# Second layer's recurrence: one 128-column product for both kinds of scores, a third scores buffer, seven parts of each inverse per chunk

## The chip, the cores and the metric

The kernel runs on one core of one Trainium2 chip. The metric is the device time of one launch in microseconds (us): 1906.67 us is the median of three runs before the change. TensorE is the matrix engine, VectorE, ScalarE and GpSimd are the three engines for elementwise work; the profile calls them PE, DVE, ACT and POOL, and TensorE's weight loads PEld.

## What is computed

One inference step of a two-layer recurrent decoder trunk, for a prompt of 512 tokens and 8 samples of 4 tokens each, width 1024. The first layer mixes with GLA and HGRN2, the second with RWKV-7, 16 heads of 64. Each layer also has a SwiGLU block and a gated embedding. The change is in the recurrence of the second layer:

```python
def step(s, inp):
    r_t, lw_t, k_t, v_t, kk_t, a_t = inp
    s_kk = jnp.einsum('bhik,bhk->bhi', s, kk_t)
    s = (s * jnp.exp(lw_t)[:, :, None, :]
         - s_kk[..., :, None] * (kk_t * a_t)[..., None, :]
         + v_t[..., :, None] * k_t[..., None, :])
    return s, jnp.einsum('bhij,bhj->bhi', s, r_t)
```

## The kernel before, in words

The program is one long list of instructions for each engine, with semaphores between them, all written out by hand. Nearly all of the time is in products of 128x128 weights (line 351) that run from the embedding to the last feed-forward block; between the products of the second layer's r, k, v and those of its output weight lies the recurrence, from 1088 us to 1299 us of the span.

The recurrence treats the prompt in chunks of 64 tokens (`CP`), so there are 8, and the samples as a ninth, `SAMPLE`. It is in the form that turns 64 steps into products of matrices. For each chunk m and each of the 16 heads there are two kinds of keys (`keys_p(tile, b)`: b = 1 the removal keys kk·a, b = 0 the keys k) and two kinds of query (`qrF[:, tile, 0]` the kk, `qrF[:, tile, 1]` the r). Their products are the scores; the triangular matrix of removal keys against kk has to be inverted. The work of a chunk is in two pieces.

**The stream** (`pe_stream`, `dve_stream`, `act_stream`, `pool_stream`) is what does not need the state. It is a list of parts, `parts_of(m)`:
- `aT`: 16 products of 64 columns, the scores of the removal keys against kk (line 2452). VectorE takes the first level of the inverse out of them and transposes it (lines 2646 and 2650), ScalarE copies the whole (line 2581).
- `P` and `X` for the levels 2 to 6: the inverse is built by doubling its blocks. P (line 2462, 16 products of 32 columns) waits for ScalarE's copy of the level before; VectorE merges it under a mask (`level_factor`, line 2661, after a transpose on line 2667); X (line 2505, 16 products) waits for that; ScalarE writes it back (line 2615; line 2620 at the last level), and GpSimd makes the copy with the halves swapped (line 2743) that the next transpose reads.
- `A`: 16 products, scores of k against kk (line 2468), which VectorE masks into `sAs` (line 2715).
- `O`: 32 products, both kinds of keys against r (line 2473), which VectorE masks into `sOs` in two instructions (line 2721).
- `vt` and `kt`: transposes of the values and keys (lines 2479 and 2482), copied out by ScalarE and VectorE.

**The chunk** (`pe_chunk` and its like) is what goes through the state: `av` (line 2768), the state against kk (R, line 2776) and against r (oR, line 2783), the inverse applied (U, line 2791), the output from the scores `sOs` (line 2803), the new state (line 2809). After each of these stands a slot, `go_on(0)` to `go_on(6)`, in which `in_chunk` puts parts of streams: "o" is the next part of the stream of chunk n+1, "n" that of chunk n+2. `HEAD` is the number of parts by which the stream n+1 is ahead when chunk n begins. A stream has 15 parts: 8 are done as "n" and 7 as "o". All engines go through the same slots in the same order, each with its own share of a part.

Each stream has two banks of PSUM, streams of even and odd chunks different ones (`bank_of`), so most parts wait until the part before has been read out; P and X use columns apart.

## Time and profile before

| | |
|---|---|
| median of 3 runs | 1906.67 us (1904.36 to 1910.46) |
| the profiled execution: its time, and its span | 1911.56 us, 1909.8 us |
| PE busy | 1761.2 us (92%) |
| PE weight loads busy | 1665.2 us (87%) |
| DVE, ACT, POOL busy | 981.6, 725.0, 217.8 us |
| mean TensorE clock | 0.937 of full |

The span is the time from the first to the last instruction that the profiler saw; the run's time is 1.8 us more. Busy time is a mean over stages of different kinds; the recurrence has windows of its own below. In the profile one 16-product part of fp32 stands as 32 matmul and 32 weight-load records.

### The profile page before, as it was taken

Reading aid. Unit: us, or ns where it says so; the run is one execution under the profiler, and the core shown is the slowest. Engines: PE = TensorE matmul, PEld = TensorE weight load, DVE = VectorE, ACT = ScalarE, POOL = GpSimd, SP = SyncE. Lnnn points to the kernel's source line nnn. Section 1 sums busy time; section 2 is a strip of 40 time slices with the busy share of each in tenths; the row PEclk is TensorE's granted clock in tenths of the full one; section 3 lists DMA queues with packets and bytes.
Section 4 is the critical chain, followed back from the end, with each engine's and each line's share of the span. In section 5 each row is a group of like instructions: output and inputs, shape, how many; then the busy total and the mean of one; then the engine's idle time right before and its main releaser. Section 6 shows DMA issues by size and latency. Waiting matters only on the chain.

```text
span 1909.8 us, 43023 instructions
## 1 busy us (share of the span) xinstructions
PE 1761.2 (92%) x18617; PEld 1665.2 (87%) x18617; DVE 981.6 (51%) x1407; ACT 725.0 (38%) x953; POOL 217.8 (11%) x307
## 2 busy tenths in 40 slices
PE   7999879799999999997999877779899999999997
PEld 6999876799999999997888767765599999999997
DVE  4487775644433444456788544433644442444444
ACT  4353444354522222333466223223445531222243
POOL 1042551000000000120060111112100000000000
PEclk8999989899999999998999878886799999999999
DMA  4321131332332333330222200010143232233321
GB/s 130 82 74 47 55 102 52 89 111 88 92 96 66 88 88 102 88 89 23 79 67 74 73 3 4 4 49 1 32 107 113 86 108 78 68 88 101 88 67 58
DMA packets 234669, 138.95 MB, mean 73 GB/s; under 512 B 4720, under 2 KB 229360, under 8 KB 234528
## 3 DMA queue, kind: packets, MB, share of 16 engines
q1 hardware_dynamic: 226784, 116.73, 21.2%
q0 software_dynamic: 4864, 15.90, 3.3%
q10 hardware_dynamic: 2880, 4.21, 0.6%
q8 instruction: 116, 1.90, 0.4%
q14 instruction: 25, 0.20, 0.0%
HBM read 128.66 MB, written 8.16 MB: 72 GB/s over the span
## 4 chain that ended last, share of the span: by engine, by line
PE 80%; DVE 9%; ACT 4%; issue 3%; POOL 2%; DMA 1%; ACTq 0%; SPq 0%; DVEq 0%; POOLq 0%
PE ps L351 62%; PE ps L1881 2%; PE ps L2505 1%; PE ps L1628 1%; ACT w_head L315 1%; DVE w_rest L320 1%; PE ps L2462 1%; PE ps L1862 1%; PE ps L2803 1%; POOL mix L984 1%; PE ps L1093 1%; PE ps L1169 1%; PE ps L2809 1%; PE ps L1900 1%; PE ps L3004 1%
## 5 line engine op out<-in xcount | busy, mean ns | idle before, releaser
L351 PE MATMUL ps<-x_split,w_head 128*128 128x272 f32 (+1 forms) x5312 | 900.0, 292 | 24.7 <-DVE x_split L1418 8.6
L351 PEld LDWEIGHTS ps<-x_split,w_head 128*128 128x128 f32 x5312 | 763.6, 191 | 38.5 <-issue 27.7
L351 PE MATMUL ps<-x_split,w_rest 128*128 128x272 f32 (+1 forms) x2656 | 555.5, 291 | 0.0
L315 ACT ACTIVATE w_head<-w_raw 128x1024 fp32r<-128x1024 f32 (+1 forms) x205 | 227.1, 1108 | 584.1 <-PE ps L351 566.8
L351 PEld LDWEIGHTS ps<-x_split,w_rest 128*128 128x128 f32 x2656 | 421.4, 191 | 0.0
L320 DVE TENSOR_TENSOR w_rest<-w_raw,w_head 128x1024 fp32r<-128x1024 f32 (+1 forms) x205 | 268.0, 1307 | 171.3 <-ACT w_head L315 171.2
L351 PE MATMUL ps<-hidden_split,w_head 128*128 128x272 f32 x1408 | 233.1, 287 | 0.0
L351 PEld LDWEIGHTS ps<-hidden_split,w_head 128*128 128x128 f32 x1408 | 198.0, 188 | 0.0
L351 PE MATMUL ps<-hidden_split,w_rest 128*128 128x272 f32 x704 | 145.3, 287 | 0.0
L1459 DVE TENSOR_TENSOR hT<-hT,ps 128x544 f32<-128x544 f32 (+1 forms) x40 | 28.8, 721 | 161.1 <-PE ps L351 161.1
L351 PEld LDWEIGHTS ps<-hidden_split,w_rest 128*128 128x128 f32 x704 | 110.0, 188 | 0.0
L1592 DVE TENSOR_TENSOR mix<-mix,ps 128x544 f32<-128x544 f32 x44 | 31.7, 721 | 127.7 <-PE ps L351 127.7
L1588 DVE TENSOR_TENSOR mix<-mix,ps 128x544 f32<-128x544 f32 x44 | 31.7, 721 | 63.8 <-PE ps L351 57.5
L1578 ACT ACTIVATE hidden_split<-mix 128x544 f32 (+1 forms) x44 | 29.0, 659 | 91.3 <-DVE mix L1596 91.3
L1762 POOL DMA_DIRECT2D out_y_prompt<-mix x4 | 2.2, 551 | 483.4 <-ACT mix L1706 483.3
L1598 DVE TENSOR_TENSOR hidden_split<-mix,hidden_split 128x544 f32 (+1 forms) x44 | 31.9, 725 | 42.5 <-ACT hidden_split L1578 42.5
L984 POOL TENSOR_TENSOR mix<-mix 128x256 f32<-128x256 f32 (+1 forms) x36 | 32.0, 890 | 176.6 <-DVE mix L1011 88.8
L1827 POOL DMA_DIRECT2D tables<-in_odd_tables x1 | 0.6, 563 | 449.7 <-PE ps L351 449.7
L1093 PE MATMUL ps<-mix 64*64 64x64 f32 (+1 forms) x896 | 36.6, 229 | 8.1 <-DVE mix L1011 8.1
L315 ACT ACT_TABLE_LOAD x20 | 25.7, 1283 | 40.6 <-PE ps L351 40.6
L1093 PEld LDWEIGHTS ps<-mix 64*64 64x64 f32 (+1 forms) x896 | 30.7, 140 | 11.6 <-DVE mix L1011 9.2
L2462 PE MATMUL ps<-odd_quad 64*64 64x32 f32 x1280 | 32.7, 245 | 7.3 <-issue 5.0
(454 smaller groups left out, 2136.5 us busy)
## 6 DMA issues: line engine op xcount, KB each, us to landing
w_raw<-in_w_ffn_gate SPq DMA_DIRECT2D x44, 512.0 KB, 3.7
w_raw<-in_w_ffn_up SPq DMA_DIRECT2D x44, 512.0 KB, 3.7
w_raw<-in_w_ffn_down SPq DMA_DIRECT2D x32, 704.0 KB, 4.7
w_raw<-in_w_in_even SPq DMA_DIRECT2D x29, 512.0 KB, 3.7
w_raw<-in_w_ple_gate SPq DMA_DIRECT2D x16, 512.0 KB, 3.9
w_raw<-in_w_out_even SPq DMA_DIRECT2D x8, 512.0 KB, 4.0
w_raw<-in_rw_wr SPq DMA_DIRECT2D x8, 512.0 KB, 3.8
w_raw<-in_rw_wk SPq DMA_DIRECT2D x8, 512.0 KB, 3.9
```

The costliest lines, as they stand in the source:

```text
L315: act.activation(wh[:, s, 0:kt * P], raw[:, s, 0:kt * P], ACT.Copy).then_inc(head_ok[s], 1)
L320: dve.tensor_tensor(wl[:, s, 0:kt * P], raw[:, s, 0:kt * P], wh[:, s, 0:kt * P].bitcast(F32), ALU.subtract).then_inc(rest_ok[s], 1)
L351: mm = pe.matmul(ps[:, 2 * s + h, 0:half.stop - half.start], w[:, s, k * P:(k + 1) * P], x[:, k, half], start=first and k == 0, stop=k == ...
L984: pool.tensor_tensor(e[:, :, 0, :], mid, b[:, :, 0, :], ALU.subtract)
L1093: mm = pe.matmul(ps[64 * (c % 2):64 * (c % 2) + CE, b0 + level // 2, at:at + CE], left[:, c * CE:(c + 1) * CE], right[:, c * CE:(c + 1) * CE],
L1459: dve.tensor_tensor(h, h, out2(s), ALU.add).then_inc(bank_free[s], 1)
L1578: act.activation(hid[:, 0, ds(j, 1), :], prod.unsqueeze(1), ACT.Copy).then_inc(hhead_ok, 1)
L1588: dve.tensor_tensor(two(act_out), two(norm_f.rs), out2(0), ALU.mult).then_inc(bank_free[0], 1)
L1592: dve.tensor_tensor(two(prod), two(norm_f.rs), out2(1), ALU.mult).then_inc(bank_free[1], 1)
L1598: dve.tensor_tensor(hid[:, 1, ds(j, 1), :], prod.unsqueeze(1), hid[:, 0, ds(j, 1), :].bitcast(F32), ALU.subtract).then_inc(hrest_ok, 1)
L1881: mm = pe.matmul(ps[:, 2 * s + h, 0:tokens.stop - tokens.start], w[:, s, k * P:(k + 1) * P], x[:, k, tokens], start=first and k == 0, stop ...
L2462: mm = pe.matmul(bank(1 - c)[half(1 - p ^ c), i * CO:(i + 1) * CO], aTs[par][r, swap_cols(c, i)], even_columns(xxs[par][r, swap_cols(c, i) ...
```

## The change

The parts aT, A and O become two. `scores(pe, b, bank)` makes, for one kind of keys, the product against kk and r side by side: the moving operand is `qrF[..., :, tokens]`, 2 x 64 columns. So aT (b = 1) and A (b = 0) are 16 products of 128 columns each, O is no part any more, and a stream has 14 parts. VectorE masks the scores against r in `out_scores`, two instructions of 64 partitions for each kind of keys: for b = 1 directly behind the first transpose of the inverse (named `O{m}_1`, and P of level 2 waits for it), for b = 0 behind the masking of A. As the b = 1 scores are now made two chunks ahead of their use, `sOs` gets a third buffer. HEAD is 7, and the slots are filled anew.

```diff
         aTS, bTS = low2[0][:, 0:P], [low2[0][:, P:2 * P], low2[0][:, 2 * P:3 * P]]
         xTS, xxS, ppS = (low2[1][:, k * P:(k + 1) * P] for k in range(3))
         sAs = [quad[:, 3584:4096], quad[:, 5120:5632]]
-        sOs = [quad[:, 4096:5120], quad[:, 5632:6656]]
+        sOs = [ap.rearrange("p (c x) -> p c x", c=2)[:, :, 0:512] for ap in (
+            quad[:, 4096:5120], quad[:, 5632:6656], mix[:, 25600:28672])]
         vus = [quad[:, at:at + 1024].rearrange("p (i b g v) -> p i b g v", i=4, b=2, g=2) for at in (6656, 7680)]
         sc_sample = mix[:, 25600:26112].rearrange("p (g n t) -> p g n t", g=2, n=4)
         vu_sample = mix[:, SC0 + 1024:SC0 + 1536].rearrange("p (i g v) -> p i g v", i=4, g=2)
...
                 return [("sc", 0), ("P", 2), ("X", 2), ("vt", 0), ("kt", 0)] + [("st", b) for b in range(2, NB)] + [
                     ("rts", 0)]
             parts = [("aT", 0)] + [(kind, level) for level in range(2, LEVELSP + 1) for kind in "PX"]
-            parts += [("A", 0), ("O", 0), ("vt", 0), ("kt", 0)]
+            parts += [("A", 0), ("vt", 0), ("kt", 0)]
             return parts + [("st", 0), ("st", 1)] if m == SAMPLE - 2 else parts
 
-        HEAD = 8
+        HEAD = 7
 
         def part_name(m, kind, x):
             return f"st{x}" if kind == "st" else "rts" if kind == "rts" else f"{kind}{m}_{x}"
...
 
         def in_chunk(streams, n, slot):
 
-            order = ("o", "n", "o", "on", "n", "on", "nononon")[slot]
+            order = ("on", "", "o", "on", "on", "on", "nonon")[slot]
             for who in order:
                 if who == "o" and n + 1 in streams:
                     next(streams[n + 1], None)
...
                 pe.wait_ge(*O1.dve.at("nrm"))
             par, before = m % 2, None if m < 2 else (m - 2, *parts_of(m - 2)[-1])
             tokens = slice(CP * m, CP * m + CP) if m < SAMPLE else slice(TP, T)
+
+            def scores(pe, b, bank):
+                for i, p, c in tile_heads:
+                    out = bank(1 - c)[half(p ^ b), i * 2 * CP:(i + 1) * 2 * CP].rearrange("p (s t) -> p s t", s=2)
+                    mm = pe.matmul(out, keys_p(2 * i + p, b)[half(c), m, :], qrF[half(c), 2 * i + p, :, tokens], start=True,
+                                   stop=True)
+                return mm
+
             for kind, x in parts_of(m):
                 if before is not None and (m == SAMPLE or kind not in ("P", "X")):
                     for by in readers(*before):
...
                 if m == SAMPLE and kind in ("sc", "P", "X", "vt", "kt", "rts"):
                     mm = pe_sample_part(pe, kind, bank)
                 elif kind == "aT":
-                    for i, p, c in tile_heads:
-                        mm = pe.matmul(bank(1 - c)[half(1 - p), i * CP:(i + 1) * CP], keys_p(2 * i + p, 1)[half(c), m, :],
-                                       qrF[half(c), 2 * i + p, 0, tokens], start=True, stop=True)
+                    mm = scores(pe, 1, bank)
                 elif kind == "P":
                     if x == 2:
                         pe.wait_ge(*O2.act.at(f"aT{m}_0"))
                         pe.wait_ge(*O2.dve.at(f"t{m}_2"))
+                        pe.wait_ge(*O2.dve.at(f"O{m}_1"))
                     else:
                         pe.wait_ge(*O2.act.at(f"X{m}_{x - 1}"))
                     for i, p, c in tile_heads:
...
                 elif kind == "X":
                     mm = pe_inverse(pe, m, x, bank)
                 elif kind == "A":
-                    for i, p, c in tile_heads:
-                        mm = pe.matmul(bank(c)[half(p), i * CP:(i + 1) * CP], keys_p(2 * i + p, 0)[half(c), m, :],
-                                       qrF[half(c), 2 * i + p, 0, tokens], start=True, stop=True)
-                elif kind == "O":
-                    for b in range(2):
-                        for i, p, c in tile_heads:
-                            mm = pe.matmul(bank(c)[half(p ^ b), (2 * i + p) * CP:(2 * i + p + 1) * CP],
-                                           keys_p(2 * i + p, b)[half(c), m, :], qrF[half(c), 2 * i + p, 1, tokens], start=True,
-                                           stop=True)
+                    mm = scores(pe, 0, bank)
                 elif kind == "vt":
                     for i in range(KT // 2):
                         at = 17408 + 1024 * i + P * m
...
         def both(m, wide):
             return ps[:, bank_of(m, 0):bank_of(m, 0) + 2, 0:wide]
 
+        def made_scores(m, s):
+            return both(m, 512).rearrange("p c (i s t) -> p c i s t", i=4, s=2)[:, :, :, s, :]
+
+        def out_scores(dve, m, b):
+
+            for p in range(2):
+                r = half(p ^ b)
+                mm = dve.tensor_tensor(sOs[m % 3][r].rearrange("p c (i b t) -> p c i b t", i=4, b=2)[:, :, :, p, :],
+                                       made_scores(m, 1)[r], scP[r, 1, :].unsqueeze(1).unsqueeze(1).to_broadcast([64, 2, 4, CP]),
+                                       ALU.mult)
+            return mm
+
         def act_stream(act, m):
             par = m % 2
             for kind, x in parts_of(m):
...
                         dst = rows_p[:, :, P * m:P * m + P].rearrange("p (b t) x -> p b t x", b=2)
                         src = both(m, 512).rearrange("p b (t x) -> p b t x", t=4)
                     else:
-                        dst = aTs[par].rearrange("p (c x) -> p c x", c=2)
-                        src = both(m, 256)
+                        dst, src = aTs[par].rearrange("p (c i t) -> p c i t", c=2, i=4), made_scores(m, 0)
                     act.activation(dst, src, ACT.Copy).then_inc(*O2.act.done(name))
                 if m < SAMPLE and kind == "P" and x == 2:
                     first_own_rows(act, m)
...
                 dve.wait_ge(*O2.dve.at(f"t{m - 1}_2"))
             dve.copy_predicated(first.rearrange("p (c i t) -> p c i t", c=2, i=4),
                                 level_bits[:, 0:CP].unsqueeze(1).unsqueeze(1).to_broadcast([P, 2, 4, CP]),
-                                both(m, 256).rearrange("p c (i t) -> p c i t", i=4)).then_inc(*O2.dve.done(f"Y{m}"))
+                                made_scores(m, 0)).then_inc(*O2.dve.done(f"Y{m}"))
             dve.wait_ge(*O2.dve.at(f"Y{m}"))
             dve.transpose(xxs[m % 2], first).then_inc(*O2.dve.done(f"t{m}_2"))
+            dve.wait_ge(*O2.act.at(f"aT{m}_0"))
+            if m > 2:
+                dve.wait_ge(*O2.pe.at(f"o{m - 3}"))
+            out_scores(dve, m, 1).then_inc(*O2.dve.done(f"O{m}_1"))
 
         def level_factor(dve, m, level):
 
...
                     elif m == SAMPLE:
                         dve.tensor_tensor(xTS, xTS, ps[:, bank_of(m, 0), 0:P], ALU.add).then_inc(*O2.dve.done(name))
                     elif kind == "A":
-                        dve.tensor_tensor(sAs[par].rearrange("p (c i t) -> p c i t", c=2, i=4),
-                                          both(m, 256).rearrange("p c (i t) -> p c i t", i=4),
-                                          scP[:, 0, :].unsqueeze(1).unsqueeze(1).to_broadcast([P, 2, 4, CP]), ALU.mult).then_inc(
-                            *O2.dve.done(name))
-                    elif kind == "O":
-                        for c in range(2):
-                            mm = dve.tensor_tensor(sOs[par][:, 512 * c:512 * c + 512].rearrange("p (n t) -> p n t", n=8),
-                                                   ps[:, bank_of(m, c), :].rearrange("p (n t) -> p n t", n=8),
-                                                   scP[:, 1, :].unsqueeze(1).to_broadcast([P, 8, CP]), ALU.mult)
-                        mm.then_inc(*O2.dve.done(name))
+                        dve.tensor_tensor(sAs[par].rearrange("p (c i t) -> p c i t", c=2, i=4), made_scores(m, 0),
+                                          scP[:, 0, :].unsqueeze(1).unsqueeze(1).to_broadcast([P, 2, 4, CP]), ALU.mult)
+                        out_scores(dve, m, 0).then_inc(*O2.dve.done(name))
                     else:
                         dst, src = values_in(m, 1)
                         dve.tensor_copy(dst, src).then_inc(*O2.dve.done(name))
...
                 pe_sample_chunk(pe)
                 return
             par, tokens = n % 2, slice(CP * n, CP * n + CP)
-            vu, sA, sO, xT = vus[par], sAs[par], sOs[par], xTs[par]
+            vu, sA, sO, xT = vus[par], sAs[par], sOs[n % 3], xTs[par]
             pe.wait_ge(*O2.dve.at(f"A{n}_0"))
             pe.wait_ge(*O2.dve.at(f"vt{n}_0"))
             pe.wait_ge(*O2.act.at(f"vt{n}_0"))
             for i, p, c in tile_heads:
-                mm = pe.matmul(ps[half(1 - p ^ c), 2 + c, i * NC:(i + 1) * NC], sA[half(p), head_cols(c, i)],
+                mm = pe.matmul(ps[half(1 - p ^ c), 2 + c, i * NC:(i + 1) * NC], sA[half(p), swap_cols(c, i)],
                                vu[half(p), i, p, c ^ p, :], start=i == 0, stop=n == 0, skip_group_check=True)
             mm.then_inc(*O2.pe.done(f"av{n}" if n else "R0"))
             go_on(0)
...
             go_on(3)
             pe.wait_ge(*O2.act.at(f"U{n}"))
             pe.wait_ge(*O2.dve.at(f"U{n}"))
-            pe.wait_ge(*O2.dve.at(f"O{n}_0"))
             pe.wait_ge(*O2.act.at(f"kt{n}_0"))
             if n > 0:
                 pe.wait_ge(*O2.pe.at(f"oR{n}"))
             for i, p, c in tile_heads:
                 g = c ^ p
                 pe.matmul(ps[half(g), 4 + p, 256 + i * CP:256 + (i + 1) * CP], vu[:, i, p, g, :],
-                          sO[:, 512 * c + (2 * i + p) * CP:512 * c + (2 * i + p + 1) * CP], start=n == 0 and i == 0, stop=True,
+                          sO[:, 1 - c, (2 * i + p) * CP:(2 * i + p + 1) * CP], start=n == 0 and i == 0, stop=True,
                           skip_group_check=True)
             go_on(4)
             for i, p, c in tile_heads:
```

How the change moves the work is seen in the order of the instructions. The first place is TensorE in the middle of a prompt chunk of the steady state, from the new state (line 2809 before, 2816 now) to the part that stands last ahead of the next chunk. Before:

```order
L2809 MATMUL ps<-odd_quad,mix 64x64 x16
L2468 MATMUL ps<-mix 64x64 x16
L2462 MATMUL ps<-odd_quad 64x32 x16
L2505 MATMUL ps<-mix,odd_quad 64x32 x16
L2473 MATMUL ps<-mix 64x64 x32
L2462 MATMUL ps<-odd_quad 64x32 x16
L2479 MATMUL ps<-ident,mix 128x128 x4
L2505 MATMUL ps<-mix,odd_quad 64x32 x16
L2482 MATMUL ps<-ident,mix 128x128 x8
L2462 MATMUL ps<-odd_quad 64x32 x16
```

Now:

```order
L2816 MATMUL ps<-odd_quad,mix 64x64 x16
L2448 MATMUL ps<-mix 64x128 x16
L2470 MATMUL ps<-odd_quad 64x32 x16
L2505 MATMUL ps<-mix,odd_quad 64x32 x16
L2479 MATMUL ps<-ident,mix 128x128 x4
L2470 MATMUL ps<-odd_quad 64x32 x16
L2482 MATMUL ps<-ident,mix 128x128 x8
L2505 MATMUL ps<-mix,odd_quad 64x32 x16
```

The 32 products of O are gone, A (now line 2448) has 128 columns, and P of level 5 has moved behind the next chunk's av. The second place is TensorE from av of the next chunk to the output product. Before:

```order
L2768 MATMUL ps<-odd_quad 64x64 x16
L2505 MATMUL ps<-mix,odd_quad 64x32 x16
L2776 MATMUL ps<-mix 64x64 x16
L2452 MATMUL ps<-mix 64x64 x16
L2783 MATMUL ps<-mix 64x64 x16
L2462 MATMUL ps<-odd_quad 64x32 x16
L2791 MATMUL ps<-mix,odd_quad 64x64 x16
L2505 MATMUL ps<-odd_quad,mix 64x32 x16
L2462 MATMUL ps<-odd_quad 64x32 x16
L2803 MATMUL ps<-odd_quad 64x64 x16
```

Now:

```order
L2776 MATMUL ps<-odd_quad 64x64 x16
L2470 MATMUL ps<-odd_quad 64x32 x16
L2448 MATMUL ps<-mix 64x128 x16
L2784 MATMUL ps<-mix 64x64 x16
L2791 MATMUL ps<-mix 64x64 x16
L2505 MATMUL ps<-mix,odd_quad 64x32 x16
L2799 MATMUL ps<-mix,odd_quad 64x64 x16
L2470 MATMUL ps<-odd_quad 64x32 x32
L2810 MATMUL ps<-odd_quad 64x64 x16
```

aT (line 2448 with 128 columns) stands ahead of both products with the state; between its end and P of level 2 (the second half of the row of 32) stand R, oR, X of level 5, U and P of level 6. The third place is VectorE in the same chunk, from the first level of the inverse of chunk n+2 to the masks of A. Before:

```order
L2646 COPY_PREDICATED mix<-odd_levels_on_chip,ps 128x512
L2650 STREAM_TRANSPOSE odd_quad<-mix 128x512
L2667 STREAM_TRANSPOSE odd_quad<-odd_quad 128x512
L2661 COPY_PREDICATED mix<-odd_levels_on_chip,ps 128x8x32
L2881 COPY odd_quad<-ps 64x2x4x64
L2661 COPY_PREDICATED mix<-odd_levels_on_chip,ps 128x128x2
L2715 TENSOR_TENSOR odd_quad<-ps,tables 128x512
L2667 STREAM_TRANSPOSE odd_quad<-odd_quad 128x512
L2661 COPY_PREDICATED mix<-odd_levels_on_chip,ps 128x64x4
```

Now:

```order
L2657 COPY_PREDICATED mix<-odd_levels_on_chip,ps 128x512
L2661 STREAM_TRANSPOSE odd_quad<-mix 128x512
L2558 TENSOR_TENSOR odd_quad<-ps,tables 64x8x64 x2
L2888 COPY odd_quad<-ps 64x2x4x64
L2682 STREAM_TRANSPOSE odd_quad<-odd_quad 128x512
L2676 COPY_PREDICATED mix<-odd_levels_on_chip,ps 128x8x32
L2676 COPY_PREDICATED mix<-odd_levels_on_chip,ps 128x128x2
L2730 TENSOR_TENSOR odd_quad<-ps,tables 128x512
L2558 TENSOR_TENSOR odd_quad<-ps,tables 64x8x64 x2
L2682 STREAM_TRANSPOSE odd_quad<-odd_quad 128x512
L2676 COPY_PREDICATED mix<-odd_levels_on_chip,ps 128x64x4
```

Two masking instructions of 64 partitions (line 2558) stand ahead of the copy of U (2888), and two more between the mask of A (2730) and the transpose and merge of level 3.

## Rows read from the trace of the kernel before

**Rows 1.** The page: busy time, share of the span, instructions, of TensorE
```profile
PE 1761.2 (92%) x18617; PEld 1665.2 (87%) x18617; DVE 981.6 (51%) x1407; ACT 725.0 (38%) x953; POOL 217.8 (11%) x307
```
**Rows 2.** Windows: length, busy (records) of PE, PEld, DVE, ACT, POOL, clock, DMA
```profile
1088.10:1119.60 31.50, 24.01 (x716) 22.00 (x716) 13.94 (x24) 5.82 (x15) 7.25 (x22) 0.50 0.08 16
1119.60:1250.07 130.47, 100.55 (x3865) 90.87 (x3864) 64.83 (x108) 41.43 (x86) 24.33 (x73) 0.86 0.02 4
1138.92:1162.31 23.39, 17.83 (x666) 16.14 (x662) 10.99 (x19) 6.96 (x15) 3.91 (x12) 0.81 0.02 4
1162.31:1182.96 20.65, 16.08 (x661) 14.44 (x660) 10.96 (x18) 6.68 (x15) 3.94 (x12) 0.91 0.02 4
1250.07:1270.86 20.79, 16.11 (x551) 14.38 (x549) 9.54 (x20) 7.19 (x15) 3.03 (x5) 0.92 0.20 53
```
**Rows 3.** Waits of TensorE, 1119.6 to 1270.9 us: total us, times, longest
```profile
PE ps L2505 <- DVE mix L2661: 10.9, 13, 1.5
PE ps L2462 <- issue: 5.0, 5, 1.6
```
**Rows 4.** Timeline of the weight loads, 1166 to 1179 us: start, us, x loads, [idle]
```profile
1170.35 0.66 PEld L2803 LDWEIGHTS ps<-odd_quad 128*64 128x64 f32 x20 [1.39 <-issue]
1171.08 0.56 PEld L2505 LDWEIGHTS ps<-mix,odd_quad 64*64 64x64 f32 x32
1171.67 1.01 PEld L2809 LDWEIGHTS ps<-odd_quad,mix 128*64 128x64 f32 x32
1172.76 0.56 PEld L2468 LDWEIGHTS ps<-mix 64*64 64x64 f32 x32
1173.22 0.33 PEld L2462 LDWEIGHTS ps<-odd_quad 64*64 64x64 f32 x11
1174.18 0.43 PEld L2462 LDWEIGHTS ps<-odd_quad 64*64 64x64 f32 x21 [0.64 <-issue]
1175.25 0.56 PEld L2505 LDWEIGHTS ps<-mix,odd_quad 64*64 64x64 f32 x32 [0.64 <-DVE mix L2661]
1175.71 1.03 PEld L2473 LDWEIGHTS ps<-mix 64*64 64x64 f32 x64
1176.81 0.30 PEld L2462 LDWEIGHTS ps<-odd_quad 64*64 64x64 f32 x11
1178.35 0.43 PEld L2462 LDWEIGHTS ps<-odd_quad 64*64 64x64 f32 x21 [1.24 <-issue]
```
**Rows 5.** DMA queues, 1119.6 to 1270.9 us: packets, MB, share
```profile
q8 instruction: 34, 0.56, 1.5%
```
**Rows 6.** Timeline of PE and DVE within one chunk, full clock
```profile
1197.34 0.69 DVE L2715 TENSOR_TENSOR odd_quad<-ps,tables 128x512 f32<-128x512 f32 x1 [5.17 <-PE ps L2468]
1197.94 0.70 DVE L2667 STREAM_TRANSPOSE odd_quad<-odd_quad 128x512 f32<-128x512 f32 x1
1198.57 0.39 DVE L2661 COPY_PREDICATED mix<-odd_levels_on_chip,ps 128x256 f32<-128x256 int32 x1
...
1199.02 0.67 PE L2505 MATMUL ps<-mix,odd_quad 64*64 64x32 f32 x32 [1.11 <-DVE mix L2661]
...
1199.50 1.14 PE L2473 MATMUL ps<-mix 64*64 64x64 f32 x64
...
1200.57 0.67 PE L2462 MATMUL ps<-odd_quad 64*64 64x32 f32 x32
...
1200.72 1.29 DVE L2721 TENSOR_TENSOR odd_quad<-ps,tables 128x512 f32<-128x512 f32 x2 [0.44 <-PE ps L2473]
...
1202.06 0.66 PE L2479 MATMUL ps<-ident,mix 128*128 128x128 f32 x4 [0.83 <-DVE odd_quad L2721]
...
1210.18 0.69 DVE L2881 COPY odd_quad<-ps 64x512 f32<-64x512 f32 x1
```
**Rows 7.** Timeline of TensorE in the last prompt chunk
```profile
1277.89 1.08 PE L2487 MATMUL ps<-ident,mix 64*128 64x64 f32 x8 [0.40 <-DMA mix<-in_state_rwkv]
1278.90 1.97 PE L2803 MATMUL ps<-odd_quad 128*64 128x64 f32 x32
```

## Prediction

> **What bounds the kernel now.** I read the page first: TensorE is busy 92% of the span [rows 1], so whatever touches the other engines alone is worth nothing outside the recurrence. Next the windows, cut where a chunk's av begins. The reader should see three things there [rows 2]. The recurrence is not limited by how much TensorE computes: in six chunks of 130.47 us it is busy 100.55 us. VectorE with 64.83 us is far from full. And the granted clock is 0.86 on the mean; through the whole opening stretch it is 0.50, the lower of its two levels (1.2 GHz).
>
> So what ends TensorE's idle time? The waits name two things: VectorE's merge of a level (line 2661, 10.9 us) and "issue", idle time with nothing that the profile shows behind it [rows 3]. The timeline of the weight loads tells what issue is. It breaks in the middle of groups of identical products, where no semaphore stands, and the count between two breaks is always the same: from 1170.35 us 20+32+32+32+11 = 127 loads to the break at 1174.18, then 21+32+64+11 = 128 to the break at 1178.35 [rows 4]. These are 3.83 and 4.17 us, **31.4 ns for a pair of load and matmul**, while a group between them runs at some 17 ns a pair (32 loads busy 0.56 us). On the DMA side 34 instruction transfers of 16.5 KB ran in the 151.3 us [rows 5], about one for each 114 pairs. My reading is that TensorE outruns the delivery of its own instructions: where the clock is full, the number of instructions sets the pace, and neither columns nor VectorE. A test: the chunk at 1162.31 with clock 0.91 has 660 pairs, times 31.4 ns is 20.7 us, and it took 20.65 us. The chunk at 1138.92, clock 0.81, took 23.39 us [rows 2]; there the slow stretches come on top. Over the six chunks 3864 pairs make 121.3 of the 130.47 us.
>
> The Trainium skill says otherwise (Runtime: NRT & Kernel Launch, Instruction fetch mechanics): instructions come in blocks of 16 KiB, and crossing a boundary is a cost "mostly hidden". The size of a transfer agrees with rows 5; "mostly hidden" does not agree with the idle 0.64 to 1.39 us at each break in rows 4.
>
> **The change, step by step.**
>
> Pairs removed. aT, A and O had 16+16+32 products; they become 16+16. That is 32 products, or 64 pairs of records (O's row shows x64 [rows 6]), for each prompt chunk. For the six chunks from 1119.60 us: 6 x 64 = 384 pairs x 31.4 ns = **-12.1 us** if delivery stays the pace.
>
> Columns. The same columns are computed. 16 products of 32 columns take 0.48 us (1199.02 to 1199.50), O's 32 products of 64 take 1.07 us (1199.50 to 1200.57), so 16 of them 0.54 [rows 6]. A 128-column group has no row: it costs at least the 0.54 us of a group with as many instructions, and at most O's 1.07 us for the same columns. I take 0.9, nearer the second, since the columns are what it shares with O. Then TensorE's own work per chunk goes from 0.54+0.54+1.07 = 2.15 to 1.8 us. At 31.4 ns the 32 pairs of such a group take 1.0 us anyway, so nothing is added at full clock.
>
> VectorE. Two instructions more per chunk, five in place of three. A copy of 64 partitions costs 0.69 us, as much as one of 128 [rows 6], so out_scores costs 1.29 us a time, as the pair on line 2721 does; bounds 0.65 (half for half the partitions) and 1.4 us. VectorE goes from 10.8 (64.83/6) to some 12.1 us a chunk, still no bound by sum. Two waits matter:
> - O1 behind the first transpose. Queued behind it on VectorE are the copy of U and the merge of level 6; on TensorE, P of level 2 and the output product. From the end of aT VectorE needs about 0.15 until it starts (1200.57 to 1200.72), 0.7 and 0.7 for merge and transpose of 512 elements (as lines 2715 and 2667), and 1.29 [rows 6], 2.9 us in all, to finish O1; TensorE has R, oR, X, U, P in between, 5 x 0.48 = 2.4 us by its own pace, but 160 pairs x 31.4 ns = 5.0 us as delivered. Cost 0 at the delivered pace, 0.5 us at P without it, and up to 0.7 more at the output product, behind the copy of U.
> - O0 behind A. X of level 3 already waits 1.11 us for mask, transpose and merge [rows 6]; 1.29 us go in ahead of the transpose, so it will wait about 2.4 us. In return the wait of vt (0.83 us) is gone. While TensorE waits, instructions arrive, which the dense stretch behind then uses; what can't be stored is lost. Bounds 0 and 1.29 us; I take a quarter, **0.3 us a chunk, +1.8 us**.
>
> The third buffer takes nothing away and lets O1 be written without waiting: the chunk that it waits for is past. ScalarE copies aT now before the R of the chunk; its wait for VectorE is hidden by the same 5 us.
>
> Opening stretch, 31.50 us at clock 0.50, thus not paced by delivery (716 pairs are 22.5 us) [rows 2]. At half clock a TensorE group costs twice its row of rows 6. O1 stands ahead of P twice: 2 x 1.29. aT of 128 columns costs 2 x (0.9-0.54) = 0.7 us more, the second, partly covered, about half of that: together +3.7. On the other side the path from A to vt was 1.07+0.69+2.14+1.29 = 5.2 and becomes 1.8+0.69+1.29 = 3.8: -1.4; one P of 0.96 us goes out of the stretch. **+1.3 us**, bounds 0 and +3.
>
> Last two chunks. From 1250 us fewer pairs (549 in 20.79 us, 17.2 us at 31.4 ns) [rows 2], so delivery doesn't pace it; there the chain of state loads does. The third state part comes O's 1.07 us earlier, call it 1.0. Its load and the load after that are a fixed chain, at the end of which the last state part waits 0.40 us on its DMA [rows 7]; now it stands behind the output product instead of ahead of it, which takes 1.97 us at half clock [rows 7], some 1.8 before the next group. **-2.8 us**, bounds -1 and -3.5.
>
> Sum: -12.1 + 1.8 + 1.3 - 2.8 = **-11.8 us** on the profiled execution's 1911.56, so 1899.8 us; that execution was 4.9 us above the median of 1906.67, so the median should be **1894.9 us**.
>
> **Rivals.**
>
> *Delivery is no bound (B).* Take the breaks away and other waits stand in their place, so that only groups and chains count: -0.35 of columns, -0.83 at vt, +1.29 at X of level 3, +0.1 us a chunk. 6 x 0.1 + 1.3 - 2.8 = -0.9 us: 1905.8. For it: 10.9 us of waits are on VectorE [rows 3], more than on the breaks of any one line. Against: the same count between breaks [rows 4], and 660 pairs at 31.4 ns filling a whole chunk [rows 2]. Chance 0.17. This is also where the rule of the Trainium skill quoted above would put the change.
>
> *VectorE's waits come on TensorE's path, slower (C).* The place is P of level 2 and X of level 3. Price: 1.29 at O0, 1.29 at O1 in front of U's copy, less 0.83 at vt and 0.35 of columns: +1.4 x 6 = +8.4, +1.3, -2.8: +6.9 us, 1913.6. It decides when the five groups behind aT take less than 2.9 us, under 18 ns a pair. For it: groups without a break do run at 15 to 17 ns. Against: over a chunk the mean is 31, and 160 pairs hardly ever come without a break [rows 4]. Chance 0.13.
>
> *More than forecast (D).* The stretches above the floor, 130.47-121.3 = 9.2 us, shrink by a third, the opening costs nothing, the end gives 3.5: -12.1-3-3.5 = -18.6, 1888.1. Chance 0.05.
>
> **How the numbers follow.** The forecast (A) has 0.65. Its own range is -17 to -6.5 us, 1889.7 to 1900.2: the quarter of 1.29 may be three quarters (+3.9), opening and end vary by 1 to 2 each. The range is 1888 to 1907 us: it takes in A, D's value and B, and leaves out C and the edges of D and B. A difference of 0.3%, 5.7 us, is about what a measurement can tell from none, so faster means below 1901.0: A and D, 0.70; B is the same, 0.17; C is slower, 0.13.
>
> **What would show it.** In the changed profile: 64 pairs less for each chunk, some 596 in a window from av to av; breaks still 127 or 128 loads apart with about 4 us between them; fully clocked chunks of 18.7 to 19.2 us and six chunks in 118 to 122 us; X of level 3 waiting 2.2 to 2.6 us for the merge, vt not at all; a 128-column group of 0.85 to 1.07 us; out_scores 1.3 us; opening stretch of 33 us. If the breaks are gone and chunks still take 21 us, B is right; if P of level 2 waits on line 2558 in most chunks, C; if 128 columns take over 1.07 us, the columns were mis-sized.

## The result, and the profile after

The changed kernel takes 1912.59 us (median of 22 runs, 1904.94 to 1917.19) against 1905.24 us (22 runs, 1896.74 to 1931.52) for the kernel before in the same session: **ratio 1.0037, 95% interval 1.0025 to 1.0049**, some 7 us slower. A few executions of the kernel before take some 24 us more than the rest, among them the 1931.52 us here. The prediction was 1894.9 us, range 1888 to 1907. The profiled execution took 1915.4 us, its span is 1913.6 us.

The page's TensorE line of the changed kernel answers to [rows 1]: 512 matmul records fewer, 64 for each of the 8 chunks, and yet more busy time.

```profile
PE 1767.7 (92%) x18105; PEld 1671.6 (87%) x18105; DVE 995.4 (52%) x1423; ACT 723.0 (38%) x953; POOL 218.1 (11%) x307
```

Windows of the changed kernel, cut as in [rows 2] (columns as there): the opening stretch, the six chunks, chunks 1 to 3 of them (counted from 0), the last of the six, and the last two stretches up to the first row on the sample's state.

```profile
1088.36:1122.41 34.05, 23.50 (x620) 21.40 (x621) 16.27 (x27) 5.80 (x15) 7.24 (x22) 0.50 0.07 15
1122.41:1254.11 131.70, 103.97 (x3482) 94.00 (x3481) 74.71 (x119) 39.71 (x86) 24.30 (x73) 0.81 0.01 4
1143.81:1165.14 21.33, 16.19 (x601) 14.48 (x597) 12.53 (x20) 6.63 (x15) 3.91 (x12) 0.89 0.01 3
1165.14:1187.07 21.93, 17.31 (x596) 15.68 (x596) 12.57 (x20) 6.37 (x15) 3.92 (x12) 0.81 0.02 4
1187.07:1208.23 21.16, 16.91 (x596) 15.17 (x596) 12.53 (x20) 6.49 (x15) 3.92 (x12) 0.82 0.02 4
1229.46:1254.11 24.65, 19.51 (x613) 17.57 (x609) 12.57 (x20) 7.58 (x17) 5.31 (x15) 0.78 0.01 3
1254.11:1272.57 18.46, 16.66 (x510) 14.69 (x509) 10.22 (x21) 6.57 (x15) 2.21 (x4) 0.86 0.13 32
1272.57:1286.32 13.75, 9.84 (x227) 8.91 (x225) 2.77 (x4) 2.88 (x5) 2.45 (x3) 0.76 0.30 79
```

The pairs are gone as foreseen, 596 in a chunk, and the six chunks still take 131.70 us where they took 130.47. The granted clock fell from 0.86 to 0.81. VectorE does 9.9 us more.

TensorE's waits of the changed kernel in the six chunks (total us, times, longest) show what took the place of the breaks:

```profile
PE ps L2505 <- DVE mix L2676: 16.7, 6, 2.9
PE ps L2799 <- ACT mix L2861: 3.7, 5, 1.5
PE ps L2505 <- issue: 2.1, 3, 1.3
PE ps L2470 <- issue: 1.7, 4, 0.7
```

Summed by kind over the six chunks, before and after: "issue" 12.5 and 5.9 us, VectorE 15.3 (19 times) and 16.7 (6 times), ScalarE 1.2 and 4.9. The idle time under "issue" was about halved; in its place stand one wait of 2.8 us at X of level 3 in each chunk, and one for ScalarE's copy of R (line 2861), which stands behind its copy of aT now.

The timeline of TensorE and VectorE of the changed kernel around that wait:

```profile
1197.18 0.97 PE L2448 MATMUL ps<-mix 64*64 64x128 f32 x25
...
1198.93 0.61 PE L2470 MATMUL ps<-odd_quad 64*64 64x32 f32 x30
1199.16 0.69 DVE L2730 TENSOR_TENSOR odd_quad<-ps,tables 128x512 f32<-128x512 f32 x1 [4.25 <-PE ps L2448]
1199.77 1.38 DVE L2558 TENSOR_TENSOR odd_quad<-ps,tables 64x512 f32<-64x512 f32 x2
1201.18 0.71 DVE L2682 STREAM_TRANSPOSE odd_quad<-odd_quad 128x512 f32<-128x512 f32 x1
1201.92 0.43 DVE L2676 COPY_PREDICATED mix<-odd_levels_on_chip,ps 128x256 f32<-128x256 int32 x1
1202.40 1.07 PE L2505 MATMUL ps<-mix,odd_quad 64*64 64x32 f32 x32 [2.86 <-DVE mix L2676]
1203.41 1.11 PE L2479 MATMUL ps<-ident,mix 128*128 128x128 f32 x4
1204.45 1.08 PE L2470 MATMUL ps<-odd_quad 64*64 64x32 f32 x32
1205.46 1.97 PE L2482 MATMUL ps<-ident,mix 128*128 128x128 f32 x8
...
1209.94 1.81 PE L2448 MATMUL ps<-mix 64*64 64x128 f32 x32
1211.58 0.63 PE L2784 MATMUL ps<-mix 64*64 64x64 f32 x32
```

To be seen: mask of A, two masks for the scores against r, transpose and merge stand one behind the other on VectorE while TensorE is idle for 2.86 us. And then something the wait's length doesn't show: up to 1211.58 the groups of 32 records go at half their pace of [rows 6]: X lasts 1.07 us in place of 0.67, and the next group starts 1.0 us later where it was 0.48. The granted clock is at its lower level (1.2 GHz) for 9 us behind the wait, nearly half the chunk. This chunk is an average one: behind the six such waits of this profile the low stretches last 3 to 13 us. The kernel before has such stretches too, so only what came on top is new. A mean clock of 0.86 over 130.47 us is some 37 us at the lower level, 0.81 over 131.70 us is some 50.

One profile is little evidence here. Two further ones of the kernel before and one of the changed kernel were taken with the experiments. The whole recurrence took 194.4, 196.2 and 190.0 us before and 198.0 and 200.3 after. Their stages, as means:

| stage | before (3) | after (2) | change | predicted |
|---|---|---|---|---|
| opening | 31.2 | 33.9 | +2.7 | +1.3 |
| six chunks | 128.9 | 132.1 | +3.2 | -10.3 |
| last two | 33.4 | 33.2 | -0.2 | -2.8 |
| sum | 193.5 | 199.1 | +5.6 | -11.8 |

The sum agrees with the 7 us of the runs. 13.5 of the 17.4 us by which the forecast missed lie in the six chunks. Single profiles spread: the six chunks took 130.5, 131.0 and 125.3 us before and 131.7 and 132.4 after, the last two 32.4 to 34.3 before and 32.2 and 34.2 after.

The prediction had named its signs. The breaks are still there: two of them that follow each other, at 1153.50 and 1157.08, lie 128 loads apart. But no chunk of the changed kernel came near 18.7 to 19.2 us; chunks 1 to 4 take 85.65 us, 21.4 each, with about half the idle time under "issue". That is the sign that it had given for its rival B, though no more than half of it: the breaks were fewer and not gone.

### The profile page after: what moved, and what is told of

It reads as the page before. It is cut to its first block, busy times and chain, and to the rows that moved or that the text cites. A ratio compares the mean times of both kernels' runs of the same rounds, so it can differ in the third digit from the quotient of the medians.

```text
span 1913.6 us, 42019 instructions
## 1 busy us (share of the span) xinstructions
PE 1767.7 (92%) x18105; PEld 1671.6 (87%) x18105; DVE 995.4 (52%) x1423; ACT 723.0 (38%) x953; POOL 218.1 (11%) x307
## 4 chain that ended last, share of the span: by engine, by line
PE 80%; DVE 8%; ACT 5%; issue 3%; POOL 2%; DMA 1%; ACTq 0%; SPq 0%; DVEq 0%; POOLq 0%
PE ps L351 62%; PE ps L1881 2%; PE ps L1628 1%; PE ps L2448 1%; ACT w_head L315 1%; PE ps L2470 1%; DVE w_rest L320 1%; PE ps L2505 1%; PE ps L1862 1%; PE ps L2482 1%; POOL mix L984 1%; PE ps L1093 1%; PE ps L1169 1%; PE ps L1900 1%; PE ps L3011 1%
## 5 line engine op out<-in xcount | busy, mean ns | idle before, releaser
L1459 DVE TENSOR_TENSOR hT<-hT,ps 128x544 f32<-128x544 f32 (+1 forms) x40 | 28.9, 722 | 161.1 <-PE ps L351 161.1
L2505 PE MATMUL ps<-mix,odd_quad 64*64 64x32 f32 x1024 | 27.3, 256 | 17.5 <-DVE mix L2676 16.7
L2505 PEld LDWEIGHTS ps<-mix,odd_quad 64*64 64x64 f32 x1024 | 24.7, 177 | 20.4 <-DVE mix L2676 17.3
L2470 PE MATMUL ps<-odd_quad 64*64 64x32 f32 x1280 | 33.9, 254 | 8.2 <-DVE odd_quad L2558 5.4
```

What stands on the lines that cost most here:

```text
L2470: mm = pe.matmul(bank(1 - c)[half(1 - p ^ c), i * CO:(i + 1) * CO], aTs[par][r, swap_cols(c, i)], even_columns(xxs[par][r, swap_cols(c, i) ...
L2505: mm = pe.matmul(bank(1 - c)[half(1 - p), P + i * CO:P + (i + 1) * CO], still, moving, start=True, stop=True)
```

## Experiments

My theory, after the result: the delivery of instructions cost time and got cheaper, but the two b = 0 masks ahead of the transpose cost far more than the quarter of their length that I had given them, by the wait and by the clock behind it. Rivals: the number of pairs never mattered; or the clock alone does it, whatever VectorE's work is.

**1. The masks for half the price.** One mask of 128 partitions for each kind of keys, in place of two of 64 (0.69 us each). Half of the scores land in the wrong place of `sOs`; the work of all other engines is as in the changed kernel.

```diff
-            for p in range(2):
-                r = half(p ^ b)
-                mm = dve.tensor_tensor(sOs[m % 3][r]...[:, :, :, p, :], made_scores(m, 1)[r], ...[64, 2, 4, CP]), ALU.mult)
-            return mm
+            return dve.tensor_tensor(sOs[m % 3]...[:, :, :, b, :], made_scores(m, 1), ...[P, 2, 4, CP]), ALU.mult)
```

> The changed kernel, but out_scores is one instruction over 128 partitions in place of two over 64, so that half of the masked scores land in wrong or stale columns; the count of VectorE's instructions is then that of the kernel before (plus none). W: X of level 3 waits 2.2 instead of 2.87 us, 0.65 us a chunk, and the opening stretch loses 1.3 us: 1907 to 1908.5 us. C: the same, and the half-clock stretch behind the wait is shorter: 1902 to 1907 us. D: no change outside the opening, 1911 to 1913 us.

Measured: 1899.78 us, ratio 0.9983 [0.9969, 0.9996], so 0.54% under the changed kernel: 10 us, with a margin of some 3 us either way, for two masks of 0.69 us saved in each of 8 chunks. Windows of this kernel (the six chunks, then chunks 1 and 2) and its largest wait:

```profile
1120.39:1239.74 119.35, 92.90 (x3482) 83.69 (x3481) 64.82 (x107) 39.13 (x86) 24.30 (x73) 0.91 0.02 4
1140.80:1158.61 17.81, 14.13 (x598) 12.70 (x596) 10.86 (x18) 6.11 (x15) 3.92 (x12) 1.00 0.02 4
1158.61:1178.95 20.34, 15.53 (x601) 13.80 (x597) 10.97 (x18) 6.07 (x15) 3.91 (x12) 0.92 0.01 4
```
```profile
PE ps L2505 <- DVE mix L2673: 11.3, 8, 1.9
```

The six chunks fall by 12.3 us against the changed kernel's profile, to what was predicted for them (118 to 122), and one chunk runs wholly at full clock in 17.81 us. So VectorE's masks take back more than the whole loss. How much the pairs gained by themselves this doesn't tell: in the runs the kernel is 3 us faster than the one before, where 11.8 had been predicted.

**2. Which of the two masks.** The same cut for one kind of keys alone, from chunk 3 on (m > 2), the other kind left as it is.

```diff
+            if b == 0 and m > 2:
+                return dve.tensor_tensor(sOs[m % 3]...[:, :, :, b, :], made_scores(m, 1), ...[P, 2, 4, CP]), ALU.mult)
```

> The changed kernel with one mask instruction in place of two only for b = 0, the scores behind A, and only in chunks 3 to 7 (half of those scores are left stale). Theory X3 (what is on the path is the wait of X of level 3, behind the b = 0 masks): 5 x 0.65 = 3.3 us less, and up to twice that if the clock gains too: 1905 to 1909 us where the changed kernel stands at 1911 to 1912. Theory U (what is on the path is the b = 1 masks ahead of the copy of U and of the merge of level 6): no change.

> The same for b = 1 only, the masks behind the first transpose, chunks 3 to 7. Theory X3: P of level 2 doesn't wait in the profile of the changed kernel, so no change: 1911 to 1912 us. Theory U: 3.3 us less or more. If both runs together give less than 6 us of the 10.5 that one mask for both gave in all chunks, the rest lies in the opening stretch (four masks, 2.6 us) or in the clock.

Measured: b = 0 (behind A): 0.9985 [0.9970, 1.0000]; b = 1 (behind the first transpose): 1.0019 [1.0004, 1.0033]. Against the changed kernel (1.0025 to 1.0049) that is -10 us for the one and -3.4 us for the other, whose interval overlaps the changed kernel's own: an effect of the b = 1 masks is not shown. In the profiles the six chunks are 125.99 us (clock 0.87) and 131.37 us (0.82). Cutting the b = 0 masks, 5 x 0.69 = 3.4 us of work, gives back some three times its own length in the runs, some two to four times with the intervals. The two gains are not parts of a sum: -10 for five chunks of one kind alone is already what experiment 1 gave for both kinds in all eight. Windows of the b = 0 kernel, chunks 1 to 3; the second is the first in which the shorter mask is made, for the stream of chunk 3:

```profile
1143.17:1164.95 21.78, 17.36 (x596) 15.72 (x596) 12.58 (x20) 6.38 (x15) 3.91 (x12) 0.81 0.01 3
1164.95:1183.67 18.72, 14.29 (x596) 12.91 (x596) 11.64 (x19) 6.10 (x15) 3.91 (x12) 0.98 0.02 4
1183.67:1204.06 20.39, 15.97 (x603) 14.23 (x598) 11.63 (x19) 6.40 (x15) 3.92 (x12) 0.89 0.02 4
```

**3. The masks at another place.** First, the b = 0 masks one slot later, as a part of VectorE's own with no product on TensorE; second, with the two query kinds in separate columns of the bank, behind VectorE's copy of vt, where kt waits for them. The edit of the first:

```diff
-            parts += [("A", 0), ("vt", 0), ("kt", 0)]
+            parts += [("A", 0), ("O", 0), ("vt", 0), ("kt", 0)]
...
-            order = ("on", "", "o", "on", "on", "on", "nonon")[slot]
+            order = ("on", "", "o", "on", "on", "on", "nonono")[slot]
```

> The changed kernel, with the b = 0 masks taken out of A and done by VectorE behind the merge of level 3 and the state update (a part O without products), and the slots put back to the old alternation (X3, masks, P4, vt, X4, kt). Theory W (the masks ahead of the merge of level 3 are simply in the way): X of level 3 waits 1.2 instead of 2.87 us, vt waits 0.8 to 1.2 again, net 0.5 to 0.8 us a chunk over six chunks: 1907 to 1910 us. Theory C (one wait of 2.9 us is what lets the clock fall to half for the following 8 us, and that costs more than the wait itself): with two short waits the clock is as in the kernel before (0.86), and with the shorter list of products the chunk takes 19.5 to 20.5 us: 1898 to 1903 us. Theory D (delivery of instructions sets the pace, the forecast's): 596 pairs a chunk are 18.7 us, so 1895 to 1899 us.

> The changed kernel with the scores laid out in PSUM by kind of query, and the b = 0 masks behind VectorE's copy of vt; kt waits for them. W: X of level 3 waits 1.3 us, but kt now waits 1.3 to 1.6 us more, 0 gained: 1911 to 1914 us. C: the wait of 2.87 us is split into two of 1.3 to 1.6 us, the clock is higher in this stretch: 1903 to 1909 us. D: 1911 to 1913 us.

Measured: 1.0041 [1.0026, 1.0056] and 1.0014 [0.9997, 1.0031]. The first gains nothing in the runs: the wait at X of level 3 falls to 8.6 us in 9 pieces, and 5.3 us appear at P behind ScalarE's copy. Its profile has the six chunks in 127.66 us (clock 0.86), 4 us less than the changed kernel's, which twelve runs don't bear out; a single profile doesn't carry that much. The second stands some 4 us under the changed kernel, with intervals that overlap. In its profile, of an execution of 1926.65 us, X waits 7.3 us and kt 7.3 us for VectorE. A move splits the wait and does not remove it: VectorE's work stays between two parts of TensorE.

**4. What a pair costs.** P of level 5 is done twice over, which adds 32 pairs a chunk, once in each kernel. Two other things come with them: TensorE's own time for 16 products, 0.48 us at full clock [rows 6], and a later end of this P, for which VectorE's merge waits.

```diff
-                    for i, p, c in tile_heads:
+                    for i, p, c in tile_heads * (2 if x == 5 else 1):
```

> The kernel before, with the 16 products of P of level 5 done twice in each prompt chunk (same inputs, same place): 32 pairs more per chunk and nothing on another engine. D: 31.4 ns a pair, +1.0 us a chunk, +8 us in all: 1911 us or more. V: the products' own 0.48 us at full clock where they are in the way, less where the next product waits anyway: +1 to +4 us: 1904 to 1907 us.

> The changed kernel with the same 16 products done twice. D, if delivery paces this kernel too: +8 us on 1910 to 1912. V: +0 to +4 us. If the rate of delivery bounds only the kernel before (660 pairs a chunk) and not the changed one (596), this run shows less than the other by at least 3 us.

Measured: 1.0029 [1.0011, 1.0046] on the kernel before, +5.5 us for 256 pairs, some 22 ns each; 1.0081 [1.0058, 1.0104] on the changed one (6 runs), +8.4 us against its 1.0037, 33 ns each. So doubled products do cost. The interval of the first runs from 8 to 34 ns a pair. It takes in both the 31.4 ns of the prediction and the 15 ns (3.8 us in all) that the products take on TensorE by themselves, so this experiment does not separate delivery from TensorE's own time. In the changed kernel this P falls in the half-clock stretch, where a group costs 1.0 us by itself.

**5. The masks for half the price, with every score in its place.** The masked scores are kept apart by kind of keys, and the output product is split the same way, 32 products of 64 rows, so that one mask of 128 partitions serves. That adds 32 pairs a chunk, the time of 16 more products on TensorE, and a wait between the halves.

```diff
+            for b in range(2):
+                for i, p, c in tile_heads:
+                    mm = pe.matmul(..., vu[half(p ^ b), i, p, g, :], sO[half(p ^ b), 1 - c, ...], ...)
...
+                    pe.wait_ge(*O2.pe.at(f"s{n}"))
```

> The changed kernel with one masking instruction of 128 partitions for each kind of keys (two less per chunk on VectorE); the masked scores are kept apart by kind of keys, so that the output product is 32 products of 64 rows in place of 16 of 128 rows: 32 pairs more per prompt chunk. Theory V (VectorE's masks are on the path one for one, as the run with one mask instruction says: 10.5 us for 16 instructions of 0.65 us; the number of pairs is not the pace): 1899 to 1902 us, beside 1903 for the kernel before. Theory D (delivery of pairs is a pace of its own): 8 x 32 pairs x 31.4 ns = 8 us are given back: 1906 to 1909 us.

Measured: 1.0020 [1.0004, 1.0037], 7 us above experiment 1. By pairs that would be 28 ns for each of 256, but the products' own time and the wait are in it too. It stands 3 us under the changed kernel, with intervals that overlap. What the masks save, the split output takes again for the most part.

**6. Is it the wait or the clock?** Idle products behind P of level 3, in the time in which TensorE waits. First 16 of 64 rows and 256 columns in every chunk, then only from chunk 2 on, then few large ones: 3 of the whole array with 384 columns (6 pairs). The last two kinds also in the kernel before, where 8 and 2 were put in.

```diff
+                    if x == 3 and m > 1:
+                        for k in range(3):
+                            mm = pe.matmul(bank(0)[:, P:512], aTs[par][:, 0:P], xxs[par][:, 0:384], start=True, stop=True)
```

> The changed kernel with 16 idle products of 256 columns behind P of level 3, where TensorE waits 2.87 us (1.7 us of work at full clock, results read by nobody, in columns 256 to 511 of the stream's banks). W and D: the work fits into the wait or overshoots it a little at half clock, and 32 pairs more are to be delivered: 1912 to 1920 us. C: the clock stays full after the wait, the eight half-clock microseconds of each chunk become five or fewer: 1895 to 1905 us, faster although more is computed.

> The changed kernel with the 16 idle products behind P of level 3 only from chunk 2 on, since the opening stretch paid 2.3 us for them in the profile. Theory C (the clock falls behind the long wait): six chunks in 122 to 125 us in place of 131.7, clock above 0.95 there, median 1904 to 1908 us. If the earlier profile was a lucky phase of the clock: 1909 to 1912 us.

> The changed kernel with 3 idle products of the whole array (128x128 by 384 columns, 6 pairs or fewer) behind P of level 3 from chunk 2 on, while VectorE masks. If it is TensorE's fall to half clock behind the wait for X of level 3 that costs the 2.5 us a chunk, the six chunks come to 119-124 us at a clock of .93 or more, and the time to 1900-1904 us (0.997-0.999 of before), better than the 16 idle products, since few pairs are added. If it is the wait itself and the pairs, the time stays at 1.002-1.004 of before, and the six chunks at 130-132 us.

> The kernel before with 8 such idle products behind P of level 3 from chunk 2 on (16 pairs more; its X of level 3 waits 1.1 to 1.5 us there). Theory C: the clock in the recurrence rises above 0.86 and the run is 2 to 6 us faster: 1898 to 1902 us, the fastest kernel of all. Otherwise 16 pairs x 6 cost 1 to 3 us: 1905 to 1907 us.

> The kernel before with 2 such idle products from chunk 2 on. Clock theory: its chunks are partly at a lower clock too (.81 and .91 in two of them), so 0.996-0.999 of before. If delivery alone bounds it: 1.000-1.001, the few pairs added.

Measured, in this order: 1.0041 [1.0017, 1.0064], 1.0004 [0.9986, 1.0023], 1.0007 [0.9990, 1.0025]; in the kernel before 0.9991 [0.9977, 1.0004] and 1.0021 [0.9997, 1.0045]. So idle work in the wait from chunk 2 on makes the changed kernel some 6 us faster (from 1.0037; 4 us either way), although VectorE does exactly the same and X starts no sooner. In every chunk it gives nothing in the runs; 2.3 us of that lie in the opening (36.36 us in place of 34.05), and the rest is within the intervals. In the kernel before idle work does nothing that can be told, although the clock of its six chunks rises from 0.85 to 0.91 in its three profiles to 0.93 and 0.94. Timeline and two windows (chunks 1 and 3) of the kernel with 3 full products:

```profile
1195.39 2.20 PE L2474 MATMUL ps<-odd_quad 128*128 128x384 f32 x6
1198.31 0.67 PE L2508 MATMUL ps<-mix,odd_quad 64*64 64x32 f32 x32 [0.71 <-DVE mix L2679]
1198.91 0.66 PE L2482 MATMUL ps<-ident,mix 128*128 128x128 f32 x4
...
1203.43 1.16 PE L2448 MATMUL ps<-mix 64*64 64x128 f32 x30
...
1207.94 0.40 PE L2802 MATMUL ps<-mix,odd_quad 64*64 64x64 f32 x11 [0.73 <-issue]
```
```profile
1140.52:1161.43 20.91, 16.75 (x607) 13.87 (x604) 12.55 (x20) 6.13 (x15) 3.91 (x12) 1.00 0.02 4
1182.55:1202.24 19.69, 16.28 (x608) 13.61 (x604) 12.52 (x20) 6.23 (x15) 3.92 (x12) 1.00 0.02 4
```

X of level 3 still starts 2.9 us behind P's products, but the clock holds: from X to aT it takes 5.12 us (1198.31 to 1203.43), in the changed kernel 7.54 us (1202.40 to 1209.94). That should give 2.4 us a chunk. It gives about half or less: the six chunks take 124.82 us, 6.9 us under the one profile of the changed kernel, and the runs gain 5.7. The breaks come back: "issue" is 11.5 us in its six chunks, and was 5.9. My reading, which no run tests by itself, is that delivery ran on under the half-clock stretch.

**7. The same in the opening.** Two idle products of 512 columns behind aT of chunks 0 and 1, added to the changed kernel with 3 full products.

```diff
+                if kind == "aT" and m < 2:
+                    for k in range(2):
+                        pe.matmul(ps[:, 4, :], ident[:, :], qrF[:, 0, 0, 0:TP], start=True, stop=True)
```

> e_fill_full with 2 idle products of 512 columns behind aT of chunks 0 and 1 too, where the opening ran at half clock in both kernels. Clock theory: the opening falls from 34.05 to 31-33 us and the time by another 1-3 us. If the opening is bound by loads and waits: no change against e_fill_full, or 1 us more.

Measured: 1.0000 [0.9982, 1.0019], 1.3 us under the kernel with the filler alone, less than the intervals. The opening of its profile is 32.24 us (clock 0.66) against 34.05. All fillers together bring the changed kernel level with the kernel before, and not below.

**8. Both remedies together**: half masks, with the scores misplaced as in experiment 1, and 2 full idle products.

> The changed kernel with one mask of 128 partitions for each kind of keys in place of two of 64 (half of the scores against r are then masked into the wrong place), and with 2 idle products of the whole array behind P of level 3 from chunk 2 on. It adds the two parts: if VectorE's length (the wait for X of level 3) and TensorE's half clock behind it each cost time by themselves, it is 2-4 us better than the half masks alone (0.9983 of before): 0.996-0.998, chunks of 18-18.7 us at clock 1.00. If the clock costs nothing once the wait is shorter, 0.998-0.999.

Measured: 1.0002 [0.9980, 1.0024]. A miss: it was expected 2 to 4 us better than half masks alone (0.9983), and no gain shows. That it is worse is not shown either, since the intervals overlap and one run of the twelve, 1919.47 us, stands 12 us above the next. In its profile the six chunks take 124.39 us, where half masks alone took 119.35. Windows of its chunks 2 and 4, both at full clock with 602 pairs:

```profile
1158.69:1177.38 18.69, 15.62 (x605) 13.29 (x602) 11.07 (x18) 6.23 (x15) 3.93 (x12) 1.00 0.02 4
1196.75:1217.36 20.61, 16.11 (x606) 13.49 (x602) 11.00 (x18) 6.14 (x15) 3.91 (x12) 1.00 0.02 4
```

At the same clock and count one takes 1.9 us more than the other; "issue" is 11.5 us in the six chunks, and 9.5 with half masks alone. That fits a full clock being worth something only where instructions are there; why the breaks cost more in this kernel stays open.

**9. Profiles alone**, for the table above. The kernel before a second and third time, and the changed one a second time.

> The kernel before once more, for a third profile of its recurrence. If the two profiles seen (194.4 and 196.2 us from the opening to the state's last part) are slow ones, as their run times 5-7 us above the median say, a run near the median shows 187-190 us; else again 194-196.

> The changed kernel once more. Three profiles of the kernel before gave 194.4, 196.2 and 190.0 us for the recurrence, so one of after does not say enough. Expected 196-199 us, chunks of 21-22 us at a clock of .80-.85; if it comes out below 193, the loss stage by stage stays open.

The third run of the kernel before took 1904.18 us with 189.95 us in the recurrence, the second 1909.9 us with 196.18. The changed kernel's second took 1917.97 us with 200.28. Both changed profiles show the same wait, 16.7 us in 6.

## Why the prediction was wrong

**What bounds the kernel: in part right.** There were breaks after a fixed number of loads, and they shrank when pairs went. The count of instruction transfers agrees better than I had it: I divided the 3864 pairs of six chunks by transfers of a longer window. With the 549 pairs behind them it is 4413 pairs for 34 transfers [rows 5], one for 130 and not for 114. What doesn't hold is a pace of 31.4 ns wherever the clock is full. Chunks of different kernels that ran wholly at clock 1.00 took 17.81 us for 596 pairs (half masks, 29.9 ns), 18.69 for 602 (31.0), 20.40 for 662 (third profile of before, 30.8) and 20.02 for 693 (before with doubled P, 28.9), but also 19.69, 20.91 and 21.12 us for 604, up to 35 ns. Some 29 ns is the least that was seen, and the number of pairs alone doesn't give the time. The Trainium skill has the crossing of a block "mostly hidden" (Runtime: NRT & Kernel Launch, Instruction fetch mechanics). In the kernel before, 14 idle pieces under "issue" stand against some 30 blocks of 128 pairs in the six chunks, but they come to 12.5 of the 130.47 us: about half of the crossings show no idle time, and the others cost too much to be called hidden.

**Pairs removed, -12.1 us: not shown at this size.** With half masks the six chunks came to 119.35 us, 9.6 us under the mean of before and 5.9 under the quickest of its three profiles; in the runs that kernel is only 3 us faster than the one before. No experiment takes pairs away and leaves all else alone, so how much of the miss belongs to this term stays open.

**The step that failed: "O0 behind A", "I take a quarter, 0.3 us a chunk, +1.8 us".** I saw that X of level 3 would wait; I had it at about 2.4 us and it is 2.86. The quarter was the error, and the bound of 1.29 as well. I reasoned that instructions arrive during the wait and are used by a dense stretch behind it. The stretch behind was not dense, as the clock fell, for 9 us in the chunk shown: 2.4 us that stood in no term, though the kernel before has such falls too, and they were in its time already. In place of +1.8 us, halving just the b = 0 masks in five chunks gave back 10 us (6 to 14 with the intervals), three times the VectorE work that it saved. If the pairs were worth their -12.1, the step took about 15 us over the six chunks (13.5 beyond its +1.8); if they were worth less, it took less. Experiment 6 points to the clock as a part of it (6 us), and experiments 1 and 2 show that the length of VectorE's work between P and X of level 3 sets it off. The two parts don't add (experiment 8), and the split is not settled.

**O1 behind the first transpose, cost 0: nearly right in the steady chunks**, where P of level 2 does not wait; halving it gave 3.4 us, less than the intervals can tell. vt's wait is gone as said. ScalarE's copy of aT ahead of R was called hidden; U waits for R's copy behind it, 3.7 us in the six chunks.

**Columns: right.** A 128-column group takes 0.91 us at full clock, 1.74 at half; out_scores takes 1.38 us a pair, where I had 1.29.

**Opening, +1.3, is +2.7.** P of level 2 waits for the b = 1 masks twice, rows of TensorE before and in the changed kernel:

```profile
1090.91 1.08 PE L2462 MATMUL ps<-odd_quad 64*64 64x32 f32 x32 [1.67 <-DVE odd_quad L2650]
1094.59 1.93 PE L2462 MATMUL ps<-odd_quad 64*64 64x32 f32 x64 [0.68 <-DVE odd_quad L2650]
...
1093.44 1.08 PE L2470 MATMUL ps<-odd_quad 64*64 64x32 f32 x32 [3.09 <-DVE odd_quad L2558]
1099.41 1.93 PE L2470 MATMUL ps<-odd_quad 64*64 64x32 f32 x64 [2.33 <-DVE odd_quad L2558]
1118.55 1.11 PE L2479 MATMUL ps<-ident,mix 128*128 128x128 f32 x4 [2.11 <-DVE odd_quad L2558]
```

The two P wait 3.09 and 2.33 us where they waited 1.67 and 0.68. The gain on the way from A to vt is small, since vt waits 2.11 us there where it waited 1.42. The term was too low, but within its bounds of 0 and +3.

**Last two, -2.8, is -0.2**, with profiles of one kernel 2 us apart. The state parts of the last chunks, the third before, and the third, fifth and last of the changed kernel:

```profile
1265.22 0.71 PE L2487 MATMUL ps<-ident,mix 64*128 64x64 f32 x8
...
1270.27 0.71 PE L2487 MATMUL ps<-ident,mix 64*128 64x64 f32 x8 [0.60 <-ACT mix L2592]
1275.48 0.68 PE L2487 MATMUL ps<-ident,mix 64*128 64x64 f32 x8 [2.22 <-DMA mix<-in_state_rwkv]
1283.40 1.08 PE L2487 MATMUL ps<-ident,mix 64*128 64x64 f32 x8 [1.13 <-DMA mix<-in_state_rwkv]
```

Neither half of the term came in full. The third part was to come 1 us sooner; counted from the start of the stretch it comes at 16.2 us on the mean before and at 16.9 after. From there to the end of the stretch it was to be 1.8 us less; it is 17.2 before and 16.3 after, and the loads are waited for as before.

**The rivals.** C, slower at 1913.6 us with a chance of 0.13, had the side and nearly the number, with a price of 1.4 us a chunk for masks at two places. Part of that is luck: its point of decision was P of level 2, which does not wait in the steady state; X of level 3 alone was enough, and the clock behind it stood in none of its terms. B, that other waits take the place of the breaks, describes the six chunks better than my forecast did; but it gave no chunk of 17.81 us for 596 pairs, as half masks have, and in the time it missed by 7 us. The chances were wrong where I let the cover by delivery stand for a wait that I had myself put at twice its size.

## What to carry to other kernels

Work that is moved onto a dependent chain between two engines can cost its whole length there and more, here some three times; don't discount it because another bound seems to cover the wait, and look at what the waiting engine's clock does behind it. Where a kernel has both delivery breaks and waits, a term that shortens one is only worth what the other leaves: price the two together, for a whole chunk. A mask on half the partitions cost as much here as one on all (0.69 us for 512 elements each); a layout that forces two of them can eat a gain elsewhere, and the version to look for here is one in which a single mask of 128 partitions serves without more products. It was not tried, and none of the versions that keep every score in its place beats the kernel before beyond its interval.
